# High and low halves of sixteen gate weight panels: made in another stage and kept in DRAM

## What is computed

```python
z = h @ w_in                       # columns: RWKV 3360, NSA 2608, gates 2 x 1024
o_rwkv = rwkv7_time_mix(z_rwkv, ...)
o_nsa  = nsa_attention(z_nsa, ...)
merged = sigmoid(gate_rwkv) * (o_rwkv @ w_branch_rwkv) + sigmoid(gate_nsa) * (o_nsa @ w_branch_nsa)
```

## Time and profile before

| what | value |
|---|---|
| median of 3 runs | 3348.91 us (3346.2 to 3352.34) |
| the profiled execution | 3336.66 us, of which the span in the trace is 3334.9 us |
| busy share of the span | PE 87%, DVE 70%, PEld 56%, ACT 37%, POOL 24% |
| projection of the queries | from 329.8 to 422.0 us of the span |
| RWKV heads | from 2077 to about 2807 us of the span |

### The profile page before, as it was taken

How to read it: one execution, slowest core, us unless ns; L and a number is a source line. 1 busy time by engine, 2 the same in 40 slices (tenths; PEclk the granted TensorE clock), 3 DMA queues, 4 the chain that set the end, 5 groups by cost and what they waited for, 6 DMA issues and landing times. The chain is left out here.

```text
span 3334.9 us, 58001 instructions
## 1 busy us (share of the span) xinstructions
PE 2889.5 (87%) x22731; PEld 1873.7 (56%) x22731; DVE 2348.5 (70%) x4135; ACT 1235.3 (37%) x2004; POOL 810.3 (24%) x475
## 2 busy tenths in 40 slices
PE   6896989975999999999699996788888878869987
PEld 3453455545677777777355664466666654334466
DVE  4794368888888888888663675778887752567732
ACT  3232134357333333333212674444444422233221
POOL 0650045520555555554102221100000011000000
PEclk9658999987999999999899998888988878989998
DMA  3001245545999999998433212211111015133140
GB/s 124 1 1 65 93 143 171 173 185 233 380 373 365 359 365 358 367 357 300 131 88 96 76 48 74 72 41 32 31 32 31 20 54 183 67 126 101 50 139 32
DMA packets 278232, 495.03 MB, mean 148 GB/s; under 512 B 18784, under 2 KB 177120, under 8 KB 275872
## 3 DMA queue, kind: packets, MB, share of 16 engines
q1 hardware_dynamic: 241184, 358.24, 31.6%
q0 software_dynamic: 36864, 134.23, 10.3%
HBM read 435.21 MB, written 57.21 MB: 148 GB/s over the span
## 5 line engine op out<-in xcount | busy, mean ns | idle before, releaser
L1347 PE MATMUL banks<-gated_hi,v_hi 128*128 128x384 bf16 (+2 forms) x1536 | 335.0, 273 | 0.5 <-DVE gated_lo L1318 0.5
L1347 PE MATMUL banks<-gated_lo,v_hi 128*128 128x384 bf16 (+2 forms) x1536 | 335.0, 273 | 0.0
L1347 PE MATMUL banks<-gated_hi,v_lo 128*128 128x384 bf16 (+2 forms) x1536 | 335.0, 273 | 0.0
L1185 POOL DMA_INDIRECT gathered_u<-in_u_rows,first_tile_rows x128 | 211.6, 1653 | 288.5 <-DVE gathered_dots L1293 156.5
L815 POOL TENSOR_TENSOR early_u_lo<-early_u_raw,early_u_hi 128x1024 bf16<-128x1024 f32 x64 | 156.1, 2439 | 336.1 <-ACT early_u_hi L875 336.1
L1190 POOL DMA_INDIRECT gathered_v<-in_v,first_tile_rows x128 | 175.3, 1369 | 202.5 <-DVE x_tokens L1285 182.7
L1771 POOL TENSOR_TENSOR gates_w_lo<-gates_raw,gates_w_hi 128x1024 bf16<-128x1024 f32 x24 | 51.3, 2141 | 644.1 <-ACT gates_w_hi L2046 644.1
L1347 PEld LDWEIGHTS banks<-gated_hi,v_hi 128*128 128x128 bf16 x1536 | 150.3, 98 | 56.3 <-issue 0.8
L846 PE MATMUL banks<-act_hi,early_u_hi 128*128 128x384 bf16 x512 | 168.0, 328 | 12.2 <-POOL early_u_lo L815 11.7
L1334 PE MATMUL banks<-act_hi,u_hi 128*128 128x384 bf16 x512 | 168.1, 328 | 11.6 <-DVE u_lo L1271 11.6
L1285 DVE SCALAR_TENSOR_TENSOR x_tokens<-gathered_v,gathered_weights,x_tokens 128x1024 f32<-128x1024 f32 x128 | 164.1, 1282 | 6.1 <-issue 2.2
(11 more groups left out here) (589 smaller groups left out, 8018.9 us busy)
## 6 DMA issues: line engine op xcount, KB each, us to landing
v_raw<-in_v SPq DMA_DIRECT2D x128, 512.0 KB
early_u_raw<-in_u SPq DMA_DIRECT2D x64, 512.0 KB, 3.6
u_raw<-in_u SPq DMA_DIRECT2D x64, 512.0 KB
gate_tables<-gate_piece SPq DMA_DIRECT2D x12, 2048.0 KB, 6.3
gate_group<-gate_tables SPq DMA_DIRECT2D x32, 768.0 KB
ffn_up_raw<-in_ffn_up SPq DMA_DIRECT2D x20, 1024.0 KB, 7.5
early_gelu<-early_gelu_columns SPq DMA_DIRECT2D x64, 192.0 KB, 1.9
gelu_early_rows<-early_gelu SPq DMA_DIRECT2D x32, 384.0 KB
```

Of the source, the lines that this page charges most:

```text
L1185: pool.indirect_dma_start(gu[:, n % GROUP, :], None, u_table, bass.IndirectOffsetOnAxis(ap=rows.index[:, 0, n:n + 1], axis=0)).then_inc(gu ...
L1347: m = pe.matmul(ps[:, bank, to:to + width], v[:, j, cols], w[:, j, tok:tok + width], start=start and n == 0 and to == 0, stop=stop and n = ...
```

## The change

Three things are new. A class `GateParts` loads the 16 gate panels during the projection of the queries, has ScalarE make the high and GpSimd the low part, and stores both to a DRAM tensor `gate_weight_parts`; its work is hung into `stream_product` by the argument `split`. In `rwkv_heads`, the panels 0 to 15 are loaded from this tensor straight into a buffer `gates_w` of three slots and multiplied as soon as they have landed; only the eight branch panels keep the two passes, now with two raw buffers. And `block_one` gets one more `k.clear_semaphores()` ahead of the experts.

```diff
@@ stream_product
+            if split is not None:
+                @block.gpsimd
+                def _(pool):
+                    for p in range(split.count):
+                        split.low(pool, p)
...
                 if beside is not None:
                     beside(sp)
+                if split is not None:
+                    for p in range(split.RAW):
+                        split.load(sp, p)
                 each(sp, load, 2)
+                if split is not None:
+                    for p in range(split.count):
+                        split.store(sp, p)
+                        if p + split.RAW < split.count:
+                            split.load(sp, p + split.RAW)
+                    split.finish(sp)
...
                     act.copy(wh[:, slot, :, 0:r.width], raw[:, slot, :, 0:r.width]).then_inc(hi_done, 1)
+                    if split is not None:
+                        for p in split.beside_chunk(c):
+                            split.high(act, p)
@@
+class GateParts:
+    RAW = 3
...
+        self.raw = sb("gate_parts_raw", [P, self.RAW, KD, P])
+        self.parts = sb("gate_parts", [P, 2, 2, KD, P], BF16)
...
+    def beside_chunk(self, c):
+        return {1: range(0, 2), 2: range(2, 8), 3: range(8, self.count)}.get(c, ())
+    def load(self, sp, p):
+        if p >= self.RAW:
+            sp.wait_ge(self.w_low, p - self.RAW + 1)
...
+        sp.dma_start(self.raw[:, p % self.RAW], self.w_in[:, :, first:first + P]).then_inc(self.landed[p % self.RAW], 16)
+    def high(self, act, p):
+        act.wait_ge(self.landed[p % self.RAW], 16 * (p // self.RAW + 1))
+        if p >= 2:
+            act.wait_ge(self.stored[p % 2], 16 * (p // 2))
+        act.copy(self.parts[:, p % 2, 0], self.raw[:, p % self.RAW]).then_inc(self.w_high, 1)
+    def low(self, pool, p):
+        pool.wait_ge(self.w_high, p + 1)
+        pool.tensor_tensor(self.parts[:, p % 2, 1], self.raw[:, p % self.RAW], self.parts[:, p % 2, 0],
+                           ALU.subtract).then_inc(self.w_low, 1)
+    def store(self, sp, p):
+        sp.wait_ge(self.w_low, p + 1)
+        sp.dma_start(self.k.dram["gate_parts"][p], self.parts[:, p % 2]).then_inc(self.stored[p % 2], 16)
+    def finish(self, sp):
+        for n in range(2):
+            sp.wait_ge(self.stored[n], 16 * (self.count // 2))
@@ block_one
+    k.clear_semaphores()
     experts = ExitStack()
@@ rwkv_heads
                 def load_gate(p):
                     if p >= 3:
-                        sp.wait_ge(w_low, p - 2)
...
-                    sp.dma_start(raw[:, p % 3], src).then_inc(w_landed[p % 3], 16)
+                        sp.wait_ge(multiplied, p - 2)
+                    sp.dma_start(parts[:, p % 3], k.dram["gate_parts"][p]).then_inc(w_landed[p % 3], 16)
+                def load_branch(q):
+                    if q >= 2:
+                        sp.wait_ge(w_low, q - 1)
+                    sp.dma_start(raw[:, q % 2], w_nsa[:, :, q * P:(q + 1) * P]).then_inc(branch_landed[q % 2], 16)
...
                 for p in range(2 * KD, 3 * KD):
                     store_gate(p)
-                    if p + 4 < 3 * KD:
-                        load_gate(p + 4)
+                    if p + 3 < 3 * KD:
+                        load_branch(p + 3 - 2 * KD)
...
-                for p in range(3 * KD):
-                    pool.wait_ge(w_high, p + 1)
-                    pool.tensor_tensor(wl[:, p % 2], raw[:, p % 3], wh[:, p % 2], ALU.subtract).then_inc(w_low, 1)
+                for q in range(KD):
+                    pool.wait_ge(w_high, q + 1)
+                    pool.tensor_tensor(parts[:, (2 * KD + q) % 3, 1], raw[:, q % 2], parts[:, (2 * KD + q) % 3, 0], ALU.subtract).then_inc(w_low, 1)
...
                     late(0, 0, None)
-                    gate_high(0)
-                    gate_high(1)
...
-                        if invert and s == 1 and i >= 1:
-                            gate_high(2 * i + 1)
-                        if invert and s == 4:
-                            gate_high(2 * i + 2)
+                        if invert and i == KD - 1 and s in (1, 4):
+                            branch_high(s // 4)
...
                         if m == 0:
-                            pe.wait_ge(w_low, p + 1)
+                            if p < 2 * KD:
+                                pe.wait_ge(w_landed[p % 3], 16 * (p // 3 + 1))
+                            else:
+                                pe.wait_ge(w_low, p + 1 - 2 * KD)
```

More of the change, by code:

```diff
@@ L1445, in _, with __init__, sb @@
                         pool.tensor_tensor(k.x[:, t, :], tmp[:, t, :], k.x[:, t, :], ALU.add)
+class GateParts:
+    RAW = 3
+    def __init__(self, k, ctx, count):
+        def sb(name, shape, dt=F32):
+            return ctx.enter_context(k.nc.sbuf_tensor(name, shape, dt))
+        self.k, self.count = k, count
+        self.raw = sb("gate_parts_raw", [P, self.RAW, KD, P])
+        self.parts = sb("gate_parts", [P, 2, 2, KD, P], BF16)
+        self.landed = [k.sem(f"gate_parts_landed{n}") for n in range(self.RAW)]
+        self.stored = [k.sem(f"gate_parts_stored{n}") for n in range(2)]
+        self.w_high, self.w_low = [k.sem(f"gate_parts_{s}") for s in ("high", "low")]
+        self.w_in = k.dram["w_in_2"].rearrange("(k p) n -> p k n", p=P)
+    def beside_chunk(self, c):
[3 more added lines that the diff above has]
+            sp.wait_ge(self.w_low, p - self.RAW + 1)
+        c, half = divmod(p, 2)
+        first = RW_COLS + NSA_COLS + half * D + c * P
+        sp.dma_start(self.raw[:, p % self.RAW], self.w_in[:, :, first:first + P]).then_inc(self.landed[p % self.RAW], 16)
[14 more added lines that the diff above has]
+            sp.wait_ge(self.stored[n], 16 * (self.count // 2))
 def block_one(k):
@@ L1679, in rwkv_heads @@
         w_landed = [k.sem(f"rw_gates_w_landed{n}") for n in range(3)]
+        branch_landed = [k.sem(f"rw_branch_w_landed{n}") for n in range(2)]
         w_high, w_low, multiplied, evicted = [k.sem(f"rw_gates_{n}") for n in ("w_high", "w_low", "multiplied", "evicted")]
@@ L1732, in _ @@
                 sp.dma_start(k.dram["kept_x"].rearrange("(t p) d -> p t d", p=P), k.x[:]).then_inc(spilled, 16)
-                for p in range(3):
+                for p in range(2):
                     load_gate(p)
@@ L2337, in dense @@
                         high, low = (k.xh, k.xl) if p < 2 * KD else nsa_out
-                        w, x = ((wh, high), (wh, low), (wl, high))[n]
-                        ins = pe.matmul(ps[:, dense_bank(p), :], w[:, p % 2, d, :], x[:, d, :], start=m == 0, stop=m == NM - 1)
+                        w, x = ((0, high), (0, low), (1, high))[n]
+                        ins = pe.matmul(ps[:, dense_bank(p), :], parts[:, p % 3, w, d, :], x[:, d, :], start=m == 0, stop=m == NM - 1)
                         if m == NM - 1:
```

49 lines of the change are left out of this document (23 added, 26 removed).

## The result

| kernel | median us | lowest and highest | runs |
|---|---|---|---|
| before | 3347.55 | 3344.87 to 3352.34 | 4 |
| after | 3315.26 | 3310.23 to 3318.17 | 4 |

The ratio is 0.990 (95%: 0.9883 to 0.9918). The direction and the mechanism were right, the size was not.

A forecast was written before the change was run, and what follows sets the result against it. The serial inversion loop over TensorE, ScalarE and VectorE was taken to bound the heads, GpSimd's passes stalling VectorE. Savings 10.1 + 7.0 + 1.8 + 3.7 = 22.6 us, less 0.8, gave 3327.1 us; range 3321 to 3333, 8 in 10 3316 to 3341.

The forecast's parts named there:

- The stretch of the predicated copies in turns 1 to 6: RWKV heads: VectorE's copies slowed beside GpSimd's low parts; removal saves 10.1 us at s = 1, 7.0 at s = 4.
- The rival of half the gain: Inversion steps: half of 18.9 us returns as waits for the next engine; gain 12.4 us, 3336.5; chance 0.20.
- The start of turn 0: Heads: two GpSimd passes in a row stretch VectorE's copies; without them it is done 3.7 us earlier.
- Turn 7 kept both stalls: Heads: branch panels 16 and 17 take the places of panels 15 and 16, so nothing is saved there.
- ScalarE's passes: Heads: removed high parts, 1.06 us each, counted at nothing, since ScalarE still idles 1.35 us until TensorE ends `lx`.
- The clear: Behind the output projection: the next stage starts after a semaphore clear, VectorE idling 1.16 us instead of 0.36; cost 0.8 us.
- cover for chunk 3: Query stage: chunk 3's low part ends at 390, TensorE needs it at 400.6; 10 us to spare.
- the last store: Query stage: lands at 416.3, ahead of VectorE's last copy at 422.0; 5.7 us to spare, cost nothing.
- I count nothing for it: Heads: TensorE's clock rising once its long idle times at s = 1 fall away, put at zero in the sum.
- The rival: Heads: the clock follows, each of six turns winning 2.3 us, 14 us more in all, 3313; chance 0.15.
- on the median 3348.9 - 21.8: Whole kernel: the saving summed from the trace, taken off the median of before, giving 3327.1 us.
- turn 0 from its first `lx`: Heads, step s = 4 of turn 0: the predicated copy takes 2.62 us instead of 0.69; 1.8 us saved.

The follow-up runs named there:

- act_back: After with ScalarE's 15 copies of 128 x 1024 put back at their old places, no GpSimd pass: 3310.74 us, 0.9899 to before.
- query24: After with 24 panels instead of 16 through the query stage, the eight more read by nobody: 3342.66 us, 0.9994 to before.
- control_before: Before run again unchanged: 3344.32 us, 1.0006 to before.
- the two repeats: Before and after, each run again unchanged: 3344.32 us and 3313.98 us.
- pool_back: After with 15 GpSimd passes of the old shape at the old places, ScalarE only giving the sign: 3350.79 us, 1.0023 to before.
- branch_late: After with the high parts of branch panels 0 and 1 moved from turn 7 to the start of the eighth turn: 3307.42 us, 0.9875 to before.
- late_fill2: branch_late with zero-weight matmuls filling four other TensorE waits in each turn (8, 6, 7 and 7): 3338.36 us, 0.9921 to before.

## Why the prediction was off

**Right, step by step.** The stretch of the predicated copies in turns 1 to 6 was 17.2 us for 17.1, and it passes on whole (waits of TensorE 17.6 less; a factor of 1.16 with a standard error of 0.15 in 60 turns; 1.79 us for 1.80 in the step itself). The rival of half the gain, another engine's wait in its place, is refuted. The start of turn 0 gave 3.4 for 3.7: without the two GpSimd passes VectorE's last copy ends at 2115.4 and still releases `lx`. Turn 7 kept both stalls. ScalarE's passes were worth nothing (act_back). The clear cost 0.80 us for 0.8. TensorE waited for no gate panel.

**Right by a thinner margin than worked out.** The query stage cost nothing, but with some 7 us of cover for chunk 3 instead of 10, and next to none for the last store instead of 5.7. Two terms were short: a store took 3.3 us at the median, up to 10.6, where I took 3.0; and where GpSimd's pass met VectorE's low part of a chunk, it was held up (5.42 us at chunk 3). I had asked what such a meeting costs VectorE; it was GpSimd that came second. The Trainium skill's page "SBUF — State Buffer", section "Who interferes with whom", has it so, whoever comes first keeping the port to its end; the trace agrees, with 5.42 us for 2.13. query24 shows where the cover ends.

**Wrong: two steps.** The first is "I count nothing for it", said of the clock. In before, filling the s = 1 idle time and nothing else wins 12 us, with the other fillers 17 to 18; putting only those stalls back into after costs between 5 and 41 us a run, and with the idle time filled 3. So TensorE's waits at s = 1 cost their own length and, in 16 of 18 turns, 1.4 to 3.0 us more than the same step takes in the filled kernels, for a time at 1.2 GHz behind them. Part of it comes back, since after has low stretches at other places of its turns: what is left over turns 1 to 6 is the 5 to 6 us by which they fell more than the stretch. They were 71.7 to 77.8 us long, where 75.5 to 78 were forecast. The rival had the mechanism and was given 0.15, but 2.3 us a turn was too much; that its 3313 lies near the 3315.3 measured is in part luck. The pair of turns behind it, 80.60 against 78.26 us, showed what the clock costs, not what lowers it: both turns have their s = 1 stall.

The second is "on the median 3348.9 - 21.8". A sum made on one trace was carried over to the median as if both kernels stood equally far from their traces. The profiled execution of before, 3336.7 us at a clock of 0.910, was one of its fastest: of 76 runs of before beside these experiments 6 were as fast, and the median is 3344.1. Their mean goes with the granted clock:

| clock | runs | mean us |
|---|---|---|
| up to 0.903 | 12 | 3348.1 |
| 0.904 and 0.905 | 18 | 3347.0 |
| 0.906 and 0.907 | 22 | 3344.8 |
| 0.908 and 0.909 | 17 | 3340.3 |
| 0.910 and more | 7 | 3339.6 |

The trace that I read was fast ahead of the stalls, not in them: its turns 1 to 6 take 474.6 us, those of control_before 474.0. But its prologue, from the first `state_factors` to the first `inv_t` of the heads, takes 33.5 us at a granted clock of 0.64, where control_before takes 36.9 at 0.58, and the heads begin 2.7 us earlier. The other five traces with the heads of before have 36.9 to 37.1 us there; of the 14 with the heads of after, 11 have 33.3 to 34.9 and three 37.0 to 37.3. So the change may shorten the prologue more often than not, which my sum doesn't have; by what, these runs don't show. The traces of the two repeats, both near their medians, are 28.9 us apart: 22.2 in turns 1 to 6 and 3.6 in the prologue. And the other end of the sum was high: the median of three, 3348.9, lies 4.8 us above that of the 76. The 12 us between trace and median stood in my own table and asked that question.

**The agreement of the two traces (-23.0 for -21.8) is partly luck.** Turns 1 to 6 gave 23.0 where 17.1 were forecast; turn 0 from its first `lx` gave 0.5 instead of 1.8; turn 7, the eighth turn and what follows gave back 3.0, which nothing in the change explains and which is of the size of the scatter between turns.

**Open.** What decides whether the clock falls behind a wait is not known from these runs: waits of about 2 us at the chain's first product and at the Gram products are in after as well and sometimes have low stretches behind them. pool_back is 6.5 us slower than control_before with equally many GpSimd passes up to the end of turn 7; 0.8 is the clear, the rest was not pursued. After without its additional clear was not tried, so that price is read from traces alone.

## What to carry to other kernels

Where a serial loop over engines sets the time, look for GpSimd passes beside VectorE operations that read two SBUF tiles: their stretch passes on in full, and moving the pass elsewhere, be it two lines as in branch_late, is cheap. A stall of TensorE of some 2 us in such a loop can cost more than its length, since the clock may fall behind it; price it with a term for the clock, and test that term with zero matmuls before trusting it. And hold the profiled execution against the median and its granted clock against other runs: a difference between two traces carries over to medians only if both stand at the same place in their spread.

## What the hardware showed that I had not expected

The scatter between runs goes with TensorE's granted clock, not with the amount of work: 3298.2 to 3355.8 us for one and the same kernel, late_fill2, at 0.924 to 0.926 for its three fastest runs and 0.905 to 0.909 for its five slowest. Matmuls that compute nothing won 12 to 18 us, where they stood ahead of the stalled `lx` of s = 1, and the 12 came with a lower granted clock in turns 1 to 6 (0.87 for 0.91), as the low stretches had moved to places where they cost less. And one predicated copy with its mask and data in SBUF (0.7 us) took 1.9 to 2.6 us beside a GpSimd pass of 2.1, while a GpSimd pass of 2.1 took 5.4 behind a VectorE operation of 4.4.
